# The second layer's modulation in four-tile pieces: at the begin of the first experts' stage, between its lots, and at the second experts' stage

## The reference, cut to what matters

```python
mod_l = split_cols(cond_lat @ w_mod[i] + b_mod[i], (D_MODEL,) * 6)
mod_c = split_cols(cond_ctx @ w_mod[i] + b_mod[i], (D_MODEL,) * 6)
a_lat = modulate(rmsnorm(h_lat, norm1_g[i]), mod_l[0], mod_l[1])
... mixer ...
h_lat = h_lat + mod_l[2] * o_lat
f_lat = modulate(rmsnorm(h_lat, norm2_g[i]), mod_l[3], mod_l[4])
h_lat = h_lat + mod_l[5] * peer_ffn(f_lat, ...)
```

## Time and profile before

| what | before |
|---|---|
| median of the timed runs | 4771.01 us |
| timed runs | 4769.7, 4771.01, 4795.25 us |
| the profiled execution, its own time | 4783.03 us |
| its span, first to last instruction | 4781.4 us |
| busy in the span: PE, DVE, POOL, ACT | 4179.8, 3339.1, 1767.5, 1307.1 us |
| mean granted TensorE clock, share of full speed | 0.925 |
| DMA | 1408.04 MB, mean 294 GB/s |
| SP's first DMA issue (iota) in the first experts' stage | 1136.08 us |
| its first and last write of gates issued (after lots 7 and 95) | 1241.75, 1572.95 us |
| SP's first DMA issue in the second experts' stage | 3555.48 us |
| its last write of gates issued | 3909.49 us |

### The profile page before, as it was taken

How to read it: one execution, slowest core, us unless ns; L and a number is a source line. 1 busy time by engine, 2 the same in 40 slices (tenths; PEclk the granted TensorE clock), 3 DMA queues, 4 the chain that set the end, 5 groups by cost and what they waited for, 6 DMA issues and landing times.

```text
span 4781.4 us, 53394 instructions
## 1 busy us (share of the span) xinstructions
PE 4179.8 (87%) x18407; PEld 2873.7 (60%) x18407; DVE 3339.1 (70%) x6731; ACT 1307.1 (27%) x2628; POOL 1767.5 (37%) x1652
## 2 busy tenths in 40 slices
PE   7999976694999899999999979886657779999997
PEld 3676664483676666666666645553443446666665
DVE  2466665568889677777777846775588767777776
ACT  3231311111666211111111123331214652222222
POOL 0012111022665455566565600000126655454452
PEclk8999978797999999999999989998778989999998
DMA  6966774713999999999999926888518999999995
GB/s 235 286 198 200 228 224 140 262 58 106 360 408 346 389 363 400 396 389 390 368 390 391 392 99 189 227 222 233 181 52 320 381 365 398 391 389 400 394 393 224
DMA packets 514579, 1408.04 MB, mean 294 GB/s; under 512 B 45693, under 2 KB 128893, under 8 KB 509471
## 3 DMA queue, kind: packets, MB, share of 16 engines
q1 hardware_dynamic: 330014, 733.73, 46.0%
q0 software_dynamic: 184320, 671.17, 36.2%
HBM read 1226.46 MB, written 178.26 MB: 294 GB/s over the span
## 4 chain that ended last, share of the span: by engine, by line
PE 65%; DVE 14%; DMA 10%; ACT 3%; POOL 3%; issue 3%; SPq 0%; DVEq 0%; ACTq 0%; POOLq 0%
PE ps L1840 20%; PE ps L1831 17%; DMA peer_arena<-in_peer_u 4%; PE ps L1804 3%; PE ps L1518 3%; DMA u_rows<-mixer_arena 3%; PE ps L746 3%; PE ps L1227 2%; PE ps L1232 2%; DMA expert_rows<-u_rows,peer_arena 2%; PE ps L321 2%; PE ps L749 2%; DVE expert_rows L2085 2%; PE ps L815 1%; DMA u_rows<-hidden 1%
## 5 line engine op out<-in xcount | busy, mean ns | idle before, releaser
L1787 POOL DMA_INDIRECT expert_rows<-u_rows,peer_arena x640 | 829.1, 1296 | 1052.5 <-DVE expert_rows L2085 821.8
L1831 PE MATMUL ps<-part_arena,peer_part_arena 128*128 128x384 f32 (+1 forms) x4096 | 1031.4, 334 | 37.7 <-DVE peer_part_arena L2128 25.4
L2085 DVE SCALAR_TENSOR_TENSOR expert_rows<-expert_rows,mixer_in 128x1024 f32<-128x1024 f32 x640 | 762.2, 1220 | 114.3 <-DMA expert_rows<-u_rows,peer_arena 112.0
L1794 POOL DMA_INDIRECT expert_rows<-in_peer_v,peer_arena x640 | 742.5, 1160 | 223.9 <-issue 186.5
L1831 PEld LDWEIGHTS ps<-part_arena,peer_part_arena 128*128 128x128 f32 x4096 | 699.7, 190 | 110.1 <-issue 99.0
L1840 PE MATMUL ps<-best,peer_arena 128*128 128x512 f32 x1540 | 685.3, 592 | 0.0
L1831 PE MATMUL ps<-mixer_in_parts,peer_part_arena 128*128 128x384 f32 (+1 forms) x2048 | 633.7, 309 | 0.0
L2110 DVE SCALAR_TENSOR_TENSOR peer_arena<-expert_rows,peer_arena 128x1024 f32<-128x1024 f32 x445 | 571.7, 1285 | 35.0 <-DVE peer_arena L2110 1.9
L1804 PE MATMUL ps<-expert_rows,peer_arena 128*128 128x512 f32 x768 | 387.8, 653 | 202.9 <-ACT peer_arena L1919 202.7
L1840 PEld LDWEIGHTS ps<-best,peer_arena 128*128 128x128 f32 x1540 | 285.1, 189 | 296.0 <-issue 296.0
L1571 POOL TENSOR_TENSOR part_arena<-peer_arena,part_arena 128x1024 fp32r<-128x1024 f32 x32 | 76.5, 2392 | 1007.1 <-ACT part_arena L1548 1007.1
(11 more groups left out here) (273 smaller groups left out, 6104.7 us busy)
## 6 DMA issues: line engine op xcount, KB each, us to landing
peer_arena<-in_peer_u SPq DMA_DIRECT2D x256, 512.0 KB, 12.1
best<-in_peer_v SPq DMA_DIRECT2D x154, 512.0 KB, 8.2
mixer_arena<-in_peer_u SPq DMA_DIRECT2D x272, 256.0 KB, 7.4
u_rows<-mixer_arena SPq DMA_DIRECT2D x136, 512.0 KB, 5.0
hidden<-in_peer_u SPq DMA_DIRECT2D x240, 256.0 KB, 6.2
u_rows<-hidden SPq DMA_DIRECT2D x120, 512.0 KB, 5.1
gates<-peer_arena SPq DMA_DIRECT2D x20, 2048.0 KB, 10.7
peer_arena<-in_peer_v SPq DMA_DIRECT2D x52, 512.0 KB, 7.6
```

The lines of the kernel that those rows point to most:

```text
L1787: pool.indirect_dma_start(u_ring[:, k % U_SLOTS, :], None, u_table, bass.IndirectOffsetOnAxis(u_index[s][:, m:m + 1], 0)).then_inc(u_row_i ...
L1794: pool.indirect_dma_start(v_ring[:, k % V_SLOTS, :], None, v_table, bass.IndirectOffsetOnAxis(v_index[s][:, m:m + 1], 0)).then_inc(v_row_i ...
L1831: mm = pe.matmul(ps[:, 6, 0:dense_tok], left[j % len(left)][:, c, :], right[:, c, :], start=at == 0, stop=at == len(todo) - 1)
L2085: dve.scalar_tensor_tensor(out=rows, in0=rows, scalar=1.0, in1=B.x[:, :, rows_at + s * P:rows_at + s * P + P], op0=ALU.mult, op1=ALU.mult, ...
```

## The change

The 48 tiles are made at three places. 24 of them (48 to 71) are multiplied in the first `peer` stage before anything else on PE, in six pieces of four tiles (2 MB a load), in two buffers that lie where `out` lies; ACT waits for them before its part of the lots. 16 (72 to 87) stay between the lots, one ahead of every fourth lot, so up to lot 60. The last eight (88 to 95) are multiplied in two pieces at the begin of the second `peer` stage. The results lie in the same PSUM bank side by side, and DVE adds the bias of each part after the lots. An unused semaphore of the helper goes.

```diff
@@ class ModTiles
-        self.used, self.summed, self.added = (B.sem(f"{name}_{x}") for x in ("w_used", "summed", "added"))
+        self.used, self.added = (B.sem(f"{name}_{x}") for x in ("w_used", "added"))
@@ peer
-    MOD = 6 * C
-    mod = ModTiles(B, (ar, Arena(y_tok[1])), "mod", 6 * C, 1, ps[:, 5, 0:2 * MOD]) if layer == 0 else None
+    FRONT, MOD, FRONT_EACH = (3 * C, C)[layer], (2 * C, 0)[layer], 4
+    mod = ModTiles(B, (ar, Arena(y_tok[1])), "mod", 9 * C, 1, ps[:, 5, 2 * FRONT:2 * FRONT + 2 * MOD]) if MOD else None
+    front_space = Arena(B.peer_arena)
+    front_space.at = at
+    front = ModTiles(B, (front_space, front_space), "front", (6 * C, 11 * C)[layer], FRONT_EACH, ps[:, 5, 0:2 * FRONT])
@@ sync
         sp.dma_start(iota, B.a["iota"]).then_inc(iota_in, 16)
+        for n in range(FRONT // FRONT_EACH):
+            front.load(sp, n, n % 2)
         if mod:
             for n in range(2):
                 mod.load(sp, n, n)
         for n in range(nd * P // TG):
             if mod:
-                for m in range(4 * n + 2, min(4 * n + 6, MOD)):
+                for m in range(2 * n + 2, min(2 * n + 4, MOD)):
                     mod.load(sp, m, m % 2)
@@ tensor
         if mod:
             pe.sem_inc(mod.used, 2)
             pe.wait_ge(mod.added, 1)
+        pe.sem_inc(front.used, 2)
+        for n in range(FRONT // FRONT_EACH):
+            front.multiply(pe, n, n % 2, n * FRONT_EACH)
         for a in range(AHEAD - 1):
             spread(a)
         turn(0)
         for n in range(nd):
             for x in range(LOTS):
                 at = n * LOTS + x
-                if mod and at % 2 == 0 and at // 2 < MOD:
-                    mod.multiply(pe, at // 2, at // 2 % 2, at // 2)
+                if at % 4 == 0 and at // 4 < MOD:
+                    mod.multiply(pe, at // 4, at // 4 % 2, at // 4)
                 lot(at)
@@ scalar, ahead of the lots
+        act.wait_ge(front.used, FRONT // FRONT_EACH + 2)
@@ vector, after the lots
+        dve.wait_ge(front.used, FRONT // FRONT_EACH + 2)
         if mod:
             dve.wait_ge(mod.used, MOD + 2)
+        front.add(dve, 0, FRONT)
+        if mod:
             mod.add(dve, 0, MOD)
```

## The result

The changed kernel took 4802.65 us in the median of 12 runs, the kernel before 4775.07 us; ratio 1.0051, 95% interval 1.004 to 1.0062. By this ratio it is slower by 24 us (the two medians lie 27.6 us apart), a small difference but clear of the scatter, since the interval leaves out 1. Measured once more, later, the same kernel took 4797.24 against 4777.05, ratio 1.0041, 1.0028 to 1.0055, or 20 us.

The account below looks back on a forecast made before the run. It took PE to bound the lots, with DVE or DMA close behind in some windows, and DVE's searches to set their begin. Terms -23.7 + 38.6 + 0 + 0.5 = +15.4 us on 4771.0 gave 4786, range 4756 to 4801.

Parts of the forecast that it names:

- The begin of the first stage: First experts' stage: 24 front tiles at half clock, 3.33 us each, make the fifth spread 38.6 us later; ends 32 and 45.
- The second rival: First stage's front runs at full clock, 1.68 us a tile; fifth spread 9 to 10 us late, net -14, 4757; chance 0.16.
- The third rival: First stage's front is hidden in PE's 59 us of idle time, leaving the lots' 23.7 us, 4747; chance 0.03.
- Between the lots: Lots 0 to 95 lose 32 tiles and gain 23.7 us, estimated by windows of sixteen lots; bounds 14.7 to 34.7.
- a sign of being wrong: In the lots: DVE's windows shrinking below their earlier busy times would mean the products were paced by something taken for work.
- The second stage: Second experts' stage: eight front tiles cost 0, covered by DVE's search with 5 us to spare; at most 26.6 us otherwise.
- The 0.5 us for the second add and the semaphores: DVE's second add and four semaphores more to clear: about 0.5 us.
- The sum: Whole kernel: -23.7 + 38.6 + 0 + 0.5 = +15.4 us, 4786 against the median 4771.0.
- the outcome called likeliest: Front at half clock, lots giving 15 to 35, net -3 to +24, time 4768 to 4795; chance 0.55.
- the first rival: Lots give at most 14.7, the first stage's begin costs 38.6 or up to 45: +24 to +30, 4795 to 4801; chance 0.26.
- the last write of the gates: In the first experts' stage, at 1572.95 before, forecast near 1588 in the profile after.

Follow-up runs that it names:

- warm start: Changed kernel with eight 512-column matmuls at the begin of PE's part of the first stage, while it waits for the first piece: 4801.68 us, 1.0043 to the kernel before.
- wide form: Changed kernel, first front's 24 tiles multiplied with the two-column condition stationary and 512 tile columns moving, results not taken: 4777.89 us, 1.0002 to the kernel before.
- one of four: Changed kernel with all front loads, but only the first tile of each first-stage piece multiplied: 4763.12 us, 0.9972 to the kernel before.
- front of 8: Against the kernel before: 8 tiles in the first front, 32 between the lots (ahead of every third), 8 at the second stage: 4759.74 us, ratio 0.9966.

## Why the prediction was right, by its steps

**The begin of the first stage** (+38.6, between 32 and 45) measured +41.9 and, in the second profile, +42.3. The mechanism was the forecast one in each part: two-column work at half clock, POOL held at the v gather of row 8, DVE behind it, `turn(0)` last. That the clock makes the tile long is shown by one kind of work at both levels: a tile takes 1.68 us between the lots at 1.00 and 3.43 in the front at 0.50, and in the warm start the records go from 34 to 21 in four microseconds as the clock falls. That the place does not forbid the full clock is shown by the wide form; that it depends on the kind of work and not on PE being busy, by the warm start. That PE's multiplications make most of the delay is shown by one of four: without three quarters of them 32 of the 41.9 us go, and 9.6 stay. Of the 3.3 us by which the term was too small, 2.4 are the tile (3.43 us in a long row, where I had taken 3.33 from two tiles in the earlier trace rows) and most of the rest the first piece's landing, 8.3 us after iota and not 7.7. From the first to the fifth spread it was 18.5 us forecast, 18.6 measured; so close a match is partly luck, since the gather of row 8 was issued 4.0 us after the first spread's start and not 2.8. One row was read wrongly without harm: the window 656 to 660 does not lie in the midst of the two tiles but reaches past their end at 658.77; the window 652 to 656, wholly inside them, has PE busy 4.00 us and 0.50 as well. The Trainium skill, "TensorE: Matmul & The Clock Gate", section "Part 1: The HAM clock gate", has sustained matmul activity release the throttle. These traces do not agree for two-column matmuls, 0.50 over 80 us of a fully busy PE; they agree for 512-column ones in the wide form, 0.92 and 1.00.

The second rival's own price was too low. The wide form is the run nearest to its condition, a front at the full clock, and there the front ends at 71.0 us and not near 59, the fifth spread is 19.8 us late and not 9 to 10, and the time is that of the kernel before, not 14 us less. The third rival's remark that 10 cold tiles would be free is borne out: 8 are free, 12 are not.

**Between the lots** (-23.7, between 14.7 and 34.7) measured -18.1 in the first profile and -24.4 in the second. Window by window it was right in sum and not in its parts. Lots 0 to 15 gave 7.1 where I had allowed 2.5 with a bound of 3.2: DVE's busy time, which I took for a floor, fell itself from 59.47 to 54.98 us. The prediction had named this as a sign of being wrong, and the step behind it is: the busy time of a window is not a fixed amount of work, since DVE's search can lie outside of it, as the reductions above show. The two other profiles with 16 tiles that were read in this window have 54.89 and 54.94 us, so it is not one execution's. Lots 16 to 31 and 48 to 63 gave 3.5 and 2.4 for 5.0 and 5.5, and the last sixteen 0.5 in one execution and about 6 in the other, for 6.7. That the sum fits is in part luck: windows that gave more stand against windows that gave less. I had not reckoned with the clock in the last 32 lots either. In the stretch of lots 64 to 79, which have no tiles now, it is 0.89 in every profile with 16 tiles, for 0.97 before; the 0.84 of the last sixteen is this execution's, the others have 0.87 to 0.92 there, for 0.90 before. That less work on PE is why it is lower, and what it costs, no run shows; DVE is busy 60.93 of 62.80 us in lots 64 to 79 anyway. That full DMA engines in lots 32 to 63 would be no floor was right: those two windows move 20.9 and 20.2 MB in place of 23.4 and 22.9.

**The second stage** (0, with 5 us to spare) is right: 4.07 us to spare, first spread at 39.9 for 39.8. The 0.5 us for the second add and the semaphores had no row, and no run shows it; with the second stage 0.8 us shorter to the same point, it is lost in the scatter.

**The sum** was +15.4 for a measured +24 and +20 in the two measurements; the two profiles of the stage have +23.8 and +17.8. Set on the 4771.0 that the prediction starts from, +24 is 4795, above the value and inside the range; the median itself, 4802.65, is not, until the 4 us are taken off that the kernel before took more beside it. It is also at the edge of the outcome called likeliest, -3 to +24, and of the 0.5% up to which the prediction counted a time as within. It is on the side of the first rival, whose mechanism (lots that give little) is at most a part of it: 6 of the 9 us missing in the first profile, none in the second. And the last write of the gates, forecast near 1588, did come at 1587.8, but by luck: the stage began 8.6 us sooner in that execution, and from its own begin the write is 23 us later than before, not 15.

**Why the whole change loses** is a matter of marginal prices, which the runs give and the prediction did not ask for. From 48 to 32 tiles between the lots saves 17 to 21 us (377.0 to 359.9 and 355.7), from 32 to 16 another 1 to 5 (355 in the mean), from 16 to none 4 to 7. The first is clear; the two others are as large as the scatter of 350 to 359 us between profiles. In the front the first eight tiles cost nothing, the third piece 7 us, and the other three about 12 each (fifth spread 73.1 with 12 tiles, 109.5 with 24). The 16 front tiles beyond the eighth cost 43 us and bring at most 5. The front of 8 keeps most of the gain and none of the cost: 16 us faster than before, 0.9966.

## What to carry to other kernels

Before work is moved into an engine's idle stretch, measure the stretch to the first instruction that other queues wait for, not to the end of the idle time in the profile, and take the work's duration at the clock that it will have there, from rows of the same kind of work at a place without other work around it. Then price the move by pieces: here the first pieces off the busy stretch saved most, after which the next engine took over, while the first pieces into the hole cost nothing and those beyond its end nearly their full length. A window's busy time of an engine is no floor for that window unless the same work must fall into it. When several queues stand behind one engine's work, its delay is everybody's: here one PE front held a gather by 48 us.

## What the runs showed of the hardware that I had not expected

- With 1.84 us of 512-column matmuls in every 5.12 us of an unbroken row of PE work, the granted clock stayed at 0.50 for 123 us; with nothing but 512-column matmuls at the same place it was at 0.92 and 1.00 in the second and third window of the front.
- The clock fell from 1.00 to 0.50 in windows in which PE was busy 4.00 of 4.00 us, when two-column matmuls had taken the place of 512-column ones.
- A load of 2 MB took 7.9 us from issue to landing with nothing ahead of it, and 7.7 once the gathers had stopped; the three that met gathers took 11.7, 14.1 and 13.0 (the second piece, 12.5, stood behind the first). With one of four multiplied the gathers lengthen too, from 6.0 to 12.6 us. The DMA share is 1.03 at 409 GB/s in a window that holds both kinds. That the two share one rate is argued from this, not shown.
